# Turning the cached keys on VectorE in 32x32 blocks instead of on TensorE

## The reference

```python
def _diff_combine(s, lam):
    p = jax.nn.softmax(s, axis=-1)
    p = p.reshape(B, H_C, 2, Q, K)
    return p[:, :, 0] - lam * p[:, :, 1]

def diff_attn_cached(q, k, v, kp, vp, lam):      # Q = 4 new tokens, P = 4096 past ones
    s_p = jnp.einsum('bqhd,bkhd->bhqk', q, kp) * scale    # 16 maps, d = 64
    s_n = jnp.einsum('bqhd,bkhd->bhqk', q, k) * scale     # the new tokens, causal
    a = _diff_combine(jnp.concatenate([s_p, s_n], axis=-1), lam)
    return einsum('bhqk,bkhe->bqhe', a[..., :P], vp) + einsum('bhqk,bkhe->bqhe', a[..., P:], v)
```

## Time and profile before

| | us |
|---|---|
| median of 3 runs | 2624.41 |
| lowest and highest | 2621.79, 2625.72 |
| span of the profiled execution | 2624.6 |

### The profile page before, as it was taken

How to read it: one execution, slowest core, us unless ns; L and a number is a source line. 1 busy time by engine, 2 the same in 40 slices (tenths; PEclk the granted TensorE clock), 3 DMA queues, 4 the chain that set the end, 5 groups by cost and what they waited for, 6 DMA issues and landing times.

```text
span 2624.6 us, 47024 instructions
## 1 busy us (share of the span) xinstructions
PE 2484.1 (95%) x17168; PEld 1960.5 (75%) x17168; DVE 1309.5 (50%) x2214; ACT 892.8 (34%) x2136; POOL 408.2 (16%) x239
## 2 busy tenths in 40 slices
PE   7999999999993999979999999998999999999878
PEld 6898898888883777748878888875666666666557
DVE  4656555333333466652244343345666666666543
ACT  4222121111112333332132111145666666666521
POOL 4224223323400000000013232200000000000021
PEclk9999999999995999989999999999999999999989
DMA  5233223214217499882233335179999999999683
GB/s 160 78 109 105 81 80 116 77 59 128 81 69 207 121 290 282 273 266 91 86 108 108 97 95 141 58 244 393 403 390 406 402 391 394 407 398 390 252 242 97
DMA packets 333492, 536.73 MB, mean 205 GB/s; under 512 B 30117, under 2 KB 242866, under 8 KB 330074
## 3 DMA queue, kind: packets, MB, share of 16 engines
q1 hardware_dynamic: 330226, 525.47, 57.5%
q10 hardware_dynamic: 3080, 8.82, 0.9%
HBM read 432.86 MB, written 101.22 MB: 203 GB/s over the span
## 4 chain that ended last, share of the span: by engine, by line
PE 87%; DVE 4%; DMA 2%; issue 2%; SPq 2%; ACT 1%; ACTq 1%; POOL 0%; POOLq 0%; DVEq 0%
PE at_ring L2815 8%; PE p_col L572 5%; PE p_col L574 5%; PE p_col L573 5%; PE p_gm L2275 4%; PE p_gm L2276 4%; PE p_gm L2277 4%; PE at_ssc L2844 4%; PE at_ring L2833 4%; PE p_row L613 4%; PE p_row L615 4%; PE p_row L614 4%; PE at_sc L2783 3%; PE at_ring L2805 3%; PE oa_out L1833 2%; PE oa_out L1835 2%
## 5 line engine op out<-in xcount | busy, mean ns | idle before, releaser
L2815 PE MATMUL at_ring<-ident,at_kp 128*128 128x128 f32 x2048 | 268.6, 277 | 13.1 <-DMA at_kp<-in_cache_k 8.0
L2815 PEld LDWEIGHTS at_ring<-ident,at_kp 128*128 128x128 f32 x2048 | 224.0, 141 | 57.4 <-issue 37.5
L572 PE MATMUL p_col<-h_hi,p_wqk 128*128 128x352 f32 x768 | 251.3, 327 | 1.1 <-DVEq L801 1.1
L574 PE MATMUL p_col<-h_hi,p_wqk 128*128 128x352 f32 x768 | 247.3, 322 | 0.0
L573 PE MATMUL p_col<-h_lo,p_wqk 128*128 128x352 f32 x768 | 247.1, 322 | 0.0
L2916 ACT ACTIVATE at_kT<-at_ring 128x512 f32<-128x512 f32 x384 | 218.1, 596 | 70.4 <-PE at_ring L2815 68.4
L613 PE MATMUL p_row<-p_wvz,h_hi 128*128 128x512 f32 x512 | 203.8, 398 | 3.5 <-ACT p_vst L696 3.5
L2275 PE MATMUL p_gm<-p_whl,h_hi 128*128 128x512 f32 x512 | 202.6, 396 | 0.9 <-DVE h_lo L2415 0.6
L615 PE MATMUL p_row<-p_wvz,h_lo 128*128 128x512 f32 x512 | 202.1, 395 | 0.0
L614 PE MATMUL p_row<-p_wvz,h_hi 128*128 128x512 f32 x512 | 201.3, 393 | 0.0
L2276 PE MATMUL p_gm<-p_whl,h_hi 128*128 128x512 f32 x512 | 199.8, 390 | 0.0
(11 more groups left out here) (403 smaller groups left out, 4872.1 us busy)
## 6 DMA issues: line engine op xcount, KB each, us to landing
at_kp<-in_cache_k SPq DMA_DIRECT2D x256, 512.0 KB, 7.6
at_vp<-in_cache_v SPq DMA_DIRECT2D x256, 512.0 KB, 7.5
s_qk<-p_res SPq DMA_DIRECT2D x32, 528.0 KB, 2.8
p_wst<-in_w_in_a SPq DMA_DIRECT2D x32, 512.0 KB, 3.9
p_wst<-in_w_in_a SPq DMA_DIRECT2D x64, 256.0 KB, 2.9
mx_qk<-s_qk SPq DMA_DIRECT2D x16, 1024.0 KB, 9.5
p_wst<-in_w_in_c SPq DMA_DIRECT2D x64, 256.0 KB, 4.6
s_v<-p_vst SPq DMA_DIRECT2D x64, 128.0 KB, 2.9
```

The lines of the kernel that those rows point to most:

```text
L572: pe.matmul(out[:, r, 0:TN], wx[:, 0, k, :], h_hi[:, k, at], start=k == 0, stop=False)
L574: last = pe.matmul(out[:, r, 0:TN], wx[:, 1, k, :], h_hi[:, k, at], start=False, stop=k == KD - 1)
L2815: last = pe.transpose(bank("key", n, f)[:, h * PAGE:(h + 1) * PAGE], kp[n % 2][k][:, tile:tile + P], c.ident[:])
```

## The change

- The 32 PE transposes of a page group and their eight evictions are gone. VectorE turns a whole page in one instruction, `transpose` of 128x1024 from `kp` to `kT`, which transposes each 32x32 block in its place.
- So that the blocks come out right, a key page is loaded otherwise: four DMAs, one for each 256 of the 1024 columns, into 32 partitions each. Partition i of a quarter holds the tokens i, 32 + i, 64 + i and 96 + i, with a run of 1 KB of each. After the block transposes the partitions of quarter x hold 32 dimensions of the columns 256x to 256x + 255, for all tokens.
- The head dimension of 64 thus lies in two blocks of 32, and scores are summed over four matmuls of 256 columns for each of four row groups: (page pair pp, odd or even head e). The two pairs of pages of a group are separate rows, that is two softmax streams, each with its own maximum, sum and accumulator over its half of the tokens. All 128 rows are real. Values: eight matmuls of 512 columns.
- At the end of a batch the two streams are merged: a matmul with the table `swap` brings each row the other's maximum and sum, then one small exponential and a few small VectorE operations; the pipeline is two steps longer. The accumulator starts from the new tokens' values, which now are made once a batch within the loop (`new_values`, `take_new`) instead of all ahead of it.
- Value pages from group 2 on are issued by ScalarE, in two pairs a step; SyncE issues the key quarters, and waits for VectorE's transposes (`keys_turned`).

```diff
@@ def key, value (transfers)
-            page(sp, g["cache_k"], lambda n, k: kp[n % 2][k][:], k_loaded, n, k)
+                sp.wait_ge(keys_turned, GP * (n - 2) + k + 1)
+            number = page_of(sp, n, k)
+            rows = g["cache_k"][0, bass.ds(number, 1)].rearrange("a (y i) h d -> i (a y) (h d)", i=32)
+            for x in range(4):
+                part = slice(32 * x, 32 * x + 32)
+                sp.dma_start(kp[n % 2][k][part, :].rearrange("i (y c) -> i y c", y=KB), rows[:, :, 256 * x:256 * x + 256]).then_inc(
+                    k_loaded[n % 2 * GP + k], 16)
@@ def sync
                 if s + 2 < NG:
-                    key(sp, s + 2, 0)
-                if s >= 3:
                     for k in range(GP):
-                        value(sp, s - 1, k)
-                if s + 2 < NG:
-                    for k in range(1, GP):
                         key(sp, s + 2, k)
@@ PE
-            def turn_keys(n, f):
-...
-                for h in range(4):
-                    tile = (4 * (f % 2) + h) * P
-                    last = pe.transpose(bank("key", n, f)[:, h * PAGE:(h + 1) * PAGE], kp[n % 2][k][:, tile:tile + P], c.ident[:])
+            def page_scores(n):
+                pe.wait_ge(keys_turned, GP * (n + 1))
+                if n >= 1:
+                    pe.wait_ge(p_ready, n)
+                for x in range(4):
+                    for pp, e in GROUPS:
+                        at = 32 * (2 * pp + e)
+                        keys = kT[:, n % 2, 2 * pp:2 * pp + 2, :].rearrange("p k (y f i) -> p f (k y) i", f=8, i=32)[:, 4 * e + x]
+                        last = pe.matmul(ssc[at:at + 32, 0:2 * PAGE], qz[:, n // NGB, e, x // 2, x % 2, :], keys, start=x == 0, stop=x == 3)
+                last.then_inc(s_ready, 1)
+            def swap_halves(b):
+                pe.wait_ge(mg_ready, b + 1)
+                wait_bank(pe, "swap", b, 0)
+                pe.matmul(bank("swap", b, 0)[:, 0:2], swap[:], mg[:, 0::2], start=True, stop=True).then_inc(filled, 1)
@@ ScalarE, in the order of a step
+                if 3 <= s and s - 1 < NG:
+                    value(act, s - 1, 0)
+                    value(act, s - 1, 2)
                 if rows_at(s):
                     take_rows(s - 2)
                 if weights_at(s):
                     take_out(s - 1)
-                if later:
-                    take_keys(s, 7)
+                if 3 <= s and s - 1 < NG:
+                    value(act, s - 1, 1)
+                    value(act, s - 1, 3)
@@ VectorE
+            def turn_keys(n, k):
+                dve.wait_ge(k_loaded[n % 2 * GP + k], 64 * (n // 2 + 1))
+                if n >= 2 and k == 0:
+                    dve.wait_ge(s_ready, n - 1)
+                dve.transpose(kT[:, n % 2, k, :], kp[n % 2][k][:]).then_inc(keys_turned, 1)
@@ VectorE, in the order of a step
                     mask_scores(s)
                     maximum(s, 0)
                     maximum(s, 1)
+                    turn_keys(s, 0)
                 if values_at(s):
                     add_page(s - 3)
                 if weights_at(s):
                     page_top(s - 1)
                     take_weights(s - 1)
                 if keys_at(s):
+                    turn_keys(s, 1)
                     difference(s)
-                if later:
-                    take_keys(s, 5)
-                    take_keys(s, 6)
+                    turn_keys(s, 2)
+                    turn_keys(s, 3)
```

More of the change, by code:

```diff
@@ L2609, in values_at, with batch_at, new_at, swap_at @@
             return 3 <= s <= NG + 2
-        def pick_at(s):
[L2612 to L2617, removed]
+        def batch_at(s, behind):
+            return (s - behind) // NGB if s >= behind and (s - behind) % NGB == 0 and (s - behind) // NGB < DB else None
+        def new_at(s):
+            return batch_at(s, 2)
+        def swap_at(s):
+            return batch_at(s, NGB + 3)
+        def pick_at(s):
+            return batch_at(s, NGB + 5)
         for s_ in range(LAST):
-            use_keys(s_, 0, 1)
             if values_at(s_):
@@ L2630, in attend @@
                 use("out", s_ - 1, 0, "act")
-            use_keys(s_, 6, 7)
+            if new_at(s_) is not None:
+                use("new", new_at(s_), 0, "act")
+            if swap_at(s_) is not None:
+                use("swap", swap_at(s_), 0, "dve")
             if pick_at(s_) is not None:
@@ L2744, in tensor_scores @@
             for b in range(DB):
[L2745 to L2748, removed]
+                for x in range(4):
+                    for pp, e in GROUPS:
+                        at = 32 * (2 * pp + e)
+                        last = pe.matmul(new[at:at + 32, 2, b * S:(b + 1) * S], qz[:, b, e, x // 2, x % 2, :], qk_s[:, 4 * e + x, S:2 * S],
+                                         start=x == 0, stop=x == 3)
             last.then_inc(n_scored, 1)
@@ L2755, in tensor_turn @@
             last.then_inc(n_turned, 1)
-        def tensor_values(pe):
-            pe.wait_ge(s_vg, 32)
-            pe.wait_ge(n_taken, 2)
-            for i in range(2):
-                out = new[:, 2 - 2 * i:4 - 2 * i, :].rearrange("p a n -> p (a n)")
-                for b in range(4):
-                    for j in range(JC):
-                        last = pe.matmul(out[32 * j:32 * j + 32, b * 256:(b + 1) * 256], aN[:, 4 * i + b, 32 * j:32 * j + 32],
-                                         v_s[:, j::JC, :], start=True, stop=True)
-                last.then_inc(n_valued, 1)
         def tensor(pe, turn_last):
@@ L2821, in turn_rows @@
                 wait_bank(pe, "row", n, 0)
-                for k in range(GP):
-                    last = pe.transpose(bank("row", n, 0)[:, k * PAGE:(k + 1) * PAGE], p[:, n % 2, k * PAGE:(k + 1) * PAGE], c.ident[:])
+                for k in range(2):
+                    last = pe.transpose(bank("row", n, 0)[:, k * PAGE:(k + 1) * PAGE], p[:, n % 2, k, :], c.ident[:])
                 last.then_inc(filled, 1)
@@ new lines, in new_values @@
+            def new_values(b):
+                if b == 0:
+                    pe.wait_ge(s_vg, 32)
+                    pe.wait_ge(n_taken, 2)
+                wait_bank(pe, "new", b, 0)
+                for pp, e in GROUPS:
+                    at = 32 * (2 * pp + e)
+                    v = v_s[:].rearrange("s (x e) d -> s e x d", e=2)[:, e]
+                    last = pe.matmul(bank("new", b, 0)[at:at + 32, :], aN[:, b, at:at + 32], v, start=True, stop=True)
+                last.then_inc(filled, 1)
```

278 lines of the change are left out of this document (122 added, 156 removed).

## The result

| | median us | runs | ratio to before |
|---|---|---|---|
| before | 2624.19 | 2621.79 to 2625.72 (4) | |
| after | 2957.63 | 2946.95 to 2961.56 (4) | 1.1265, 95% [1.1242, 1.1287] |

The changed kernel is 333 us slower. The prediction was 2885 (2690 to 2960): the right direction and the right mechanism, 73 us too little. The median lies only 2 us inside the upper end of the range, and two of the four runs lie above it, so that the range holds it is in part luck. Times and ratios compare runs of the faster of two states alone, which leaves one run (2854.51 us, the other took 2900.01) of the second order in set 5. The profiled execution has a span of 2959.6 us, 335.0 more than the one of before.

What follows compares the result with a forecast made beforehand. PE bound the kernel by 3.6 us a head; after the change the key transfers would. From 2624.6 us, (123.2 - 89.9) x 7.75 heads adds 258 and the tail 2: 2885 us, range 2690 to 2960.

Steps and rivals of the forecast that it cites:

- PE is the bound by 3.6 us a head only; DMA's most is 413 GB/s: Attention stage before: a head takes 89.9 us, its 35.65 MB of transfers at 413 GB/s would take 86.3 us.
- Key transposes leave PE; PE falls to 52 us a head: PE in attention: 33.4 us of key transposes a head go, leaving about 52, at most 104 at the lower clock.
- Two of four weight transposes go: -2.5 us a head: PE in attention: 16 weight transposes a head fewer, at 0.156 us each, save 2.5 us.
- Transposes of 1.22 us, VectorE 85 us a head: VectorE: 32 block transposes a head add 39 us, evictions of 11.1 go; 57.3 becomes 85, ends 72 and 128.
- Rival 2: VectorE binds because block transposes take 2.57 us: 130.5 us a head, 2941 us in total; 8 in 100.
- ScalarE: issues of 0.92 us: ScalarE drops 27 us of evictions a head and gains 32 value-page issues, 29 us, staying near 60.
- SyncE: 0.65 us an issue: SyncE's queue: 128 key issues a head instead of 32, 83 us a head, under the transfers' time.
- The transfers, the term that decides: Key quarters at 201.5 GB/s, 83.3 us a head, plus 45.7 for the rest; 123.2 taken between 93.8 and 129.0.
- Crossing from the second to the third quarter of the partitions bought nothing: Read from the sample group's t_v load, four 32-partition transfers running at 207, 213, 197 and 189 GB/s.
- Rival 1: 32 partitions cost nothing, only the 1 KB runs do: 93.8 us a head, 2657 us in total; 12 in 100.
- rival 3: Not slower: key slices move like 4 KB rows, 86.3 us a head, 2599 us in total; 5 in 100.
- Signs: Attention steps some 15 us, PE about 50 a head, VectorE waiting longest on keys, 290 GB/s, slices landing after 7 us.

Runs made afterwards that it cites:

- set 5: Changed kernel with only the order of each page's key quarters changed: 0, 2, 1, 3 took 2882.01 us; second order 0, 3, 1, 2 took 2854.51 us (one run).
- set 3: Changed kernel with each key page loaded as one transfer of whole rows and, from the third group on, only half of it turned: 2611.29 us, ratio 0.9948.
- set 4: Kernel before with only the two softmax streams and merge, keys still turned by PE: 2633.08 us; with value pages also issued by ScalarE: 2675.11 us.

## Why the prediction was right, and where its size was off

- *PE is the bound by 3.6 us a head only; DMA's most is 413 GB/s.* Right. With nothing else in the way (set 3) the stage went to 87.1 us a head at 410 GB/s, for 86.3 predicted.
- *Key transposes leave PE; PE falls to 52 us a head.* PE is busy 59.5% of 131.2, 78 us. The work that left is as predicted, but what stayed runs at a granted clock of 0.77 to 0.79: the product with the prompt's values takes 383 ns a matmul on the page, 283 before over 1800 to 2500. It lies within the 104 that the prediction bounded it by, and is covered.
- *Two of four weight transposes go: -2.5 us a head.* The 2.5 were overestimated and not netted: 13.5 us in 700 went (1.7 a head) and 14.6 came (set 4), since the prediction put the new tokens' matmuls "under PE's and ScalarE's slack" and gave the pick and the swap on PE no price. In after that slack exists; where PE is the bound it does not.
- *Transposes of 1.22 us, VectorE 85 us a head.* 1.24 us, and 64.7% of 131.2 is 85. Rival 2 is out.
- *ScalarE: issues of 0.92 us.* 1.4 us for two. Nothing in after hangs on it; with keys turned by PE it costs 42 us.
- *SyncE: 0.65 us an issue* (four in 2.70 are 0.675, 86 us a head for 83). 0.32 by the median, but 1.03 from issue to issue over the stage. It is an effect and not a cause: four transfers of the same number and size to 128 partitions went through at 2700 us.
- *The transfers, the term that decides.* Right in kind: key quarters at the rate of t_v bound the stage. Mis-sized: the prediction took 123.2 of 93.8 to 129.0 us a head, granting values on their own queue some overlap; where between these ends it put the number was a choice that no row fixed. Measured: 131.2. With the rest at 413 (45.7 us) the keys take 85.5 us, 196 GB/s for 201.5: full addition and a little more. The two queues do overlap (their shares sum to 1.06), but what one gains the other pays for. A packet of ScalarE's queue took 0.446 x 6400 us of the engines' time / 14029 = 203 ns in after, and 0.454 x 6400 / 19168 = 152 ns in the kernel of four 128-partition transfers, whose queue row is below; so the values' packets are slower with the quarters beside them.

```profile
q10 hardware_dynamic: 19168, 69.28, 45.4%
```

- *"Crossing from the second to the third quarter of the partitions bought nothing"* was read from one crossing in t_v, and wrong as a rule: an order that crosses at every step buys 76 us (103 in the one run of the other). With it the stage takes 121.6 us a head (421 quarters in 400 us), near the 123.2 that was predicted for the order which does not.
- *Sum.* 8.0 us a head too little over 7.75 heads is 62 us. The steady part of before took 89.0 a head between the same issues and not 89.9, 7 more. The slow start, which the prediction put at nothing, is 10 more, and the tail is -2 instead of +2. That is 75: 2885 + 75 = 2960, the profiled span.
- *Range.* 2960 holds 2957.63 by 2 us. The low end of 2690 does not fit its own words: 101 us a head make 2713.
- *Rival 1* (no price for 32 partitions, 2657) and *rival 3* (2599) are out by the rate, 267 to 279 GB/s. Yet rival 3's floor was real: the kernel of set 3 has it, 2611.
- *Signs.* VectorE's longest wait on key transfers, DMA share above 1, slices landing after 7.8 us, no key transposes on PE: all there. From 1904 to 2035 the steps take 13 to 21 us and do not grow with the block. The rate was 272 for 290, and PE was busy 78 us a head for about 50.

How the loss is made up, read as a ladder from kernels that differ in one thing: before 2624; transfers at their floor, half the transposes 2611; whole transposes +51; 1 KB runs +5; four transfers +33; 32 partitions each +258. The middle steps were tried only in this order, and the +5 stands under a VectorE that is the bound. No version tried computes the reference and beats before. Of the versions with VectorE's transposes that compute it, those with alternated quarters are the best, at 2882 and 2855 (one run).

## What to carry to other kernels

When an engine's work is moved by changing a layout, price the transfers that make the layout before the engines: here the stage had 4% of room in its transfers, so nothing could be won there and much be lost. Ask of each transfer how many partitions it writes and how many entries its outermost dimension has, for each of them cost a factor here (272 for 369 GB/s, and 96 for some 384; that the second comes from the outermost dimension is inferred). If narrow transfers can't be avoided, alternate them between the lower and the upper 64 partitions, and put issues on an engine whose copies no PSUM bank waits for.

## What the runs showed of the hardware that was not expected

- Order of 32-partition transfers on one queue: 0, 1, 2, 3 gave 272 GB/s with the values beside it, 0, 2, 1, 3 gave 294 and 0, 3, 1, 2 (one run) gave 303 over 1900 to 2300.
- 4 KB rows into 32 partitions are hardly faster than 1 KB runs (280 for 272 GB/s), though on 128 partitions 1 KB runs are slower than 4 KB rows (349 in the earlier trace rows for 413 in the earlier trace rows).
- With transfers whose source has 4 entries outermost the DMA share was 0.27 and the rate 96 GB/s.
- SyncE's issue of a transfer stretched from 0.32 to up to 5.4 us while quarters landed 7.8 us after their issue; the profile shows no wait then.
- The block transpose of 128x1024 float32 takes VectorE 1.24 us, of 128x512 0.70.
